# Mixer of a hybrid decoder step: state cleared in the projection phase, the norm's root one chunk earlier, and the scan's filling work in another order

## The reference

```python
zxbcdt = x @ w_in                                  # z, x/B/C, dt
xbc = silu(causal_conv(xbc, ...))                  # width 4, per channel
y, h_final = ssd_scan(xh, dt, a, bmat, cmat, h0)   # chunks of 128 tokens, state carried on
y = (y + d_skip * xh) * silu(z)
y = y * rsqrt(mean(y * y over the group) + eps) * norm_g
return y @ w_out
```

## Time and profile before

| what | us |
|---|---|
| median of 3 runs | 3813.22 (3812.39 to 3816.89) |
| the profiled execution | 3802.48 |
| its span, from the first to the last instruction | 3800.7 |
| PE busy | 3465.9 (91%) |
| DVE busy | 2221.5 (58%) |
| ACT busy | 973.7 (26%) |
| POOL busy | 997.9 (26%) |

### The profile page before, as it was taken

How to read it: one execution, slowest core, us unless ns; L and a number is a source line. 1 busy time by engine, 2 the same in 40 slices (tenths; PEclk the granted TensorE clock), 3 DMA queues, 4 the chain that set the end, 5 groups by cost and what they waited for, 6 DMA issues and landing times.

```text
span 3800.7 us, 55918 instructions
## 1 busy us (share of the span) xinstructions
PE 3465.9 (91%) x21178; PEld 3293.7 (87%) x21178; DVE 2221.5 (58%) x3463; ACT 973.7 (26%) x2300; POOL 997.9 (26%) x455
## 2 busy tenths in 40 slices
PE   7999999999996999999988888888886799999997
PEld 7888888888886999999987777777775699999997
DVE  7667767767767633333367666666666753333335
ACT  4333333433332211111113222322232211111112
POOL 3123222222211333433422111111110043333431
PEclk9999999999996999999988888888987799999997
DMA  3111111111110123211102220122110011111111
GB/s 113 36 40 59 48 40 59 42 40 59 42 42 27 45 89 134 89 51 45 45 34 75 62 61 33 44 66 61 61 50 28 12 51 45 45 50 45 45 50 51
DMA packets 85970, 200.85 MB, mean 53 GB/s; under 512 B 8920, under 2 KB 46808, under 8 KB 85248
## 3 DMA queue, kind: packets, MB, share of 16 engines
q1 hardware_dynamic: 35552, 139.54, 10.5%
q10 hardware_dynamic: 50224, 58.37, 4.9%
HBM read 166.93 MB, written 39.60 MB: 54 GB/s over the span
## 4 chain that ended last, share of the span: by engine, by line
issue 65%; PE 19%; POOLq 9%; POOL 5%; SPq 1%; DMA 0%; DVE 0%; ACT 0%; ACTq 0%; DVEq 0%
PE jb L342 19%; POOLq L317 8%; POOL wl L318 5%; SPq L297 1%; DMA wraw<-in_wstream 0%; PE aux L516 0%; ACT acc L937 0%; DVE acc L1346 0%; POOLq L325 0%; POOLq L314 0%; SPq L274 0%; SPq L280 0%; DVE lnq L1350 0%; ACT lnq L925 0%; PE aux L523 0%
## 5 line engine op out<-in xcount | busy, mean ns | idle before, releaser
L315 POOL TENSOR_TENSOR wh<-wraw,one 128x1024 fp32r<-128x1024 f32 x225 | 438.1, 1947 | 2705.7 <-PE jb L342 2253.2
L342 PE MATMUL jb<-xh,wh 128*128 128x344 f32 x2784 | 905.7, 325 | 25.0 <-issue 13.1
L342 PE MATMUL jb<-xl,wh 128*128 128x344 f32 x2784 | 892.4, 321 | 0.0
L342 PE MATMUL jb<-xh,wl 128*128 128x344 f32 x2784 | 892.1, 320 | 0.0
L1162 DVE TENSOR_TENSOR acc<-jb,acc 128x344 f32<-128x344 f32 x672 | 336.3, 515 | 473.2 <-PE jb L342 467.1
L318 POOL TENSOR_TENSOR wl<-wraw,wh 128x1024 fp32r<-128x1024 f32 x225 | 559.6, 2487 | 32.0
L342 PEld LDWEIGHTS jb<-xh,wh 128*128 128x128 f32 x2784 | 526.4, 189 | 33.3 <-issue 20.8
L342 PEld LDWEIGHTS jb<-xl,wh 128*128 128x128 f32 x2784 | 526.0, 189 | 1.7
L342 PEld LDWEIGHTS jb<-xh,wl 128*128 128x128 f32 x2784 | 526.0, 189 | 0.0
L342 PE MATMUL jb<-hh,wh 128*128 128x344 f32 x1536 | 492.2, 320 | 0.0
L342 PE MATMUL jb<-hl,wh 128*128 128x344 f32 x1536 | 490.9, 320 | 0.0
(11 more groups left out here) (251 smaller groups left out, 5658.4 us busy)
## 6 DMA issues: line engine op xcount, KB each, us to landing
wraw<-in_wstream SPq DMA_DIRECT2D x225, 512.0 KB, 3.2
pre<-in_state ACTq DMA_DIRECT2D x16, 512.0 KB, 4.2
out_ssm_s<-pre ACTq DMA_DIRECT2D x16, 512.0 KB, 3.2
kgat<-in_cache_k SPq DMA_DIRECT2D x16, 512.0 KB, 5.4
vgat<-in_cache_v SPq DMA_DIRECT2D x16, 512.0 KB, 6.4
past<-kgat ACTq DMA_DIRECT2D x8, 1024.0 KB, 5.7
past<-vgat ACTq DMA_DIRECT2D x8, 1024.0 KB, 5.9
acc<-in_xT SPq DMA_DIRECT2D x8, 516.0 KB, 7.2
```

The source lines that it names most:

```text
L315: nc.gpsimd.tensor_tensor(wh[slot][:].rearrange("p k m -> p (k m)"), wraw[:, slot].rearrange("p k m -> p (k m)"), one[:].to_broadcast([P, ...
L342: last = mm(jb[:, c, 0:CW], w[slot][:, j * kt + k], x[:, k, cols], start=(k == 0 and p == 0), stop=(k == kt - 1 and p == 2))
```

## The change

Three edits, all in the mixer.

1. Copying the group's decay factors and clearing the state `hst` (with the wait for the store of the state before) move from the head of DVE's `scan_group` to its `project_group`, behind the silu of chunk 3, at x == 4.
2. The root (ACT) and the reciprocal (DVE) of the norm move from x == 7 to x == 6. PE's part stays in its place.
3. In groups 1 to 7 the scan is filled with the six z chunks in steps 0 to 2, two each, and with the eight output blocks in steps 3 to 7 (two, one, two, two, one). Before, the output blocks stood in steps 0 to 2 (two, four, two) and the z chunks in steps 3 to 7. The stream is fetched in the new order. Group 0's filling stays.

```diff
-FILL = {0: (("o", 0), ("o", 1)), 1: (("o", 2), ("o", 3), ("o", 4), ("o", 5)), 2: (("o", 6), ("o", 7)),
-        3: (("z", 0, 0),), 4: (("z", 0, 1),), 5: (("z", 0, 2),), 6: (("z", 1, 0), ("z", 1, 1)), 7: (("z", 1, 2),)}
+FILL = {0: (("z", 0, 0), ("z", 0, 1)), 1: (("z", 0, 2), ("z", 1, 0)), 2: (("z", 1, 1), ("z", 1, 2)),
+        3: (("o", 0), ("o", 1)), 4: (("o", 2),), 5: (("o", 3), ("o", 4)), 6: (("o", 5), ("o", 6)), 7: (("o", 7),)}
...
-GROUP_ORDER = (0, 1, 2, 3, 4, 5, 6, 7)
+GROUP_ORDER = (0, 1, 2, 3, 6, 7, 4, 5)
...
-                        if x == 7 and fin:
+                        if x == 6 and fin:
                             norm_root(n - 1)
...
+            def begin_scan(n, fin):
+                nc.vector.tensor_copy(tg[:], tok[:, :, :, bass.ds(n * R, R)])
+                if fin:
+                    dve.wait_ge(s["h_out"], 16 * n)
+                nc.vector.memset(hst[:], 0.0)
+                drain().then_inc(s["h_zero"], 1)
...
                     if x:
                         silu(n, x - 1)
-                    if x == 7 and fin:
+                    if x == 4:
+                        begin_scan(n, fin)
+                    if x == 6 and fin:
                         invert(n - 1, "rms_sqrt", "rms_inv")
...
             def scan_group(at, n, out):
-                nc.vector.tensor_copy(tg[:], tok[:, :, :, bass.ds(n * R, R)])
-                if out:
-                    dve.wait_ge(s["h_out"], 16 * n)
-                nc.vector.memset(hst[:], 0.0)
-                drain().then_inc(s["h_zero"], 1)
```

## The result

The kernel before took 3815.05 us on the chip of the comparison (median of four runs, 3812.39 to 3821.64), the changed one 3854.44 us (median of four, 3843.27 to 3863.43). The ratio is 1.0117 with an interval of 1.0088 to 1.0145: the change costs 39.4 us, where the forecast had 20.9. The profiled executions took 3802.48 and 3843.27 us (spans 3800.7 and 3840.7), a difference of 40.8. One execution of the kernel before, on the chip where n1, a3, a4 and b1 ran, took 13767 us and is left out.

What follows compares the result with a forecast made beforehand. TensorE was taken to set the mixer's pace, its idle time a few recurring gaps per group. Added 77.7 less removed 56.8 gave +20.9 us, so 3823.4 profiled and 3834.1 predicted, range 3795 to 3856.

Steps and rivals of the forecast that it cites:

- L449 gone: Scan's first off-diagonal product no longer waits for the cleared state: 3.36 us per group, 23.5 us removed.
- L404 gone: The norm's spread no longer waits for the reciprocal, as the root moves earlier: 1.34 us per group, 9.4 removed.
- late bank gone: Projection: banks ScalarE frees late come in time without a z chunk in the last step; 5.9 us removed.
- wait at L432: Scan's first matmul waits for silu 9, delayed by GpSimd's split in the projection: 1.7 us (0 to 2).
- wait at L470: Scan's step 0: masked decay late after the split holds conv 11 and two silus; 2.0 us (0.5 to 3.5).
- gap ahead of o1 in step 3: VectorE's add frees the bank late, behind z gate, sample decay and GpSimd's split: 4.9 us, 5.3 at most.
- o pairs: Steps 5 and 6, two output blocks each: bank freed after it is wanted, 0.2 us each, 2.8 in all.
- loop's turn: TensorE's gap at the loop's turn, 1.25 us, was to stay as it is.
- clock at the removed wait: Slow clock (0.50) behind the wait for the cleared state goes with it: 2.1 us per group, 14.7 removed.
- covered entry: Rival: at the scan's entry conv 8 or conv 11 slips past the split, 25.9 us not added: 3808; chance 0.17.
- faster: Rival: the split's holds don't bite in step 3 either; 3772 with a covered entry; chance 0.18.
- the short gaps cost clock too: Rival: one of the new 1.7 and 2.0 us gaps leaves a slow clock, 15 us more: 3849; chance 0.13.

Runs made afterwards that it cites:

- n1: Changed kernel with the norm's root and reciprocal back at x == 7; 150.46 us per group against the changed kernel's 148.34.
- a3: Changed kernel with the split signal of the z unit in step 0 given in the middle of its second chunk; 146.63 us per group against 148.34.
- a4: Changed kernel with the split signal of the projection's last unit 2.4 us later; 150.06 us per group against 148.34.
- b1: Changed kernel with three late split signals, sample products a step earlier, second z gate, stores and output blocks moved; 3756.61 us against 3813.65 before, ratio 0.9844.
- a2: Changed kernel with the split signal of the o unit in step 3 given at its first block's third chunk; 145.93 us per group against 148.34.
- b3: The rebuilt kernel (b1) with all three split signals at their units' first matmul again; 139.46 us per group against 133.49.
- a1: Changed kernel with the sample states' stores behind ScalarE's last wait of the scan; 146.77 us per group against 148.34.
- p2: Kernel before with only the new filling and weight order; 150.41 us per group against 140.14 before.
- b5_split_later_x3: The rebuilt kernel (b1) with the last projection unit's split signal 1.0 us later; 133.30 us per group against 133.49.

## Why the prediction was right in its direction and wrong in its size

By its own steps, per group of the loop (us; a wait's price without the clock):

| step | forecast | measured |
|---|---|---|
| L449 gone | -3.36 | -3.36 |
| L404 gone | -1.34 | -1.34, by the filling, not by the root's move |
| late bank gone | -0.99 | -0.99 |
| wait at L432 | +1.7 | +1.82 |
| wait at L470 | +2.0 | +0.79 |
| gap ahead of o1 in step 3 | +4.9 | +4.75 |
| o pairs | +0.4 | +0.08 |
| loop's turn | 0 | +2.32 |
| clock at the removed wait | -2.1 | -2.28 |
| clock at the scan's entry | 0 | +2.36 |
| clock at step 3 | +2.1 | +2.19 |
| clock at the loop's turn | 0 | +1.88 |
| sum | +3.3 | +8.2 |

The clock's rows are TensorE's work at 0.50 in that part of the group (4.96 us before; 5.12, 4.76 and 4.09 after) times the 0.46 of the fit.

**Right.** The direction, and the three waits with what ends them. Step 3's gap was worked out instruction by instruction, and hit within 0.15 us. The entry's holds came as reckoned, 3.9 us on conv 8. The rivals "covered entry" and "faster" fell: the split got in between the two sample decays. This agrees with the exclusive lock of the Trainium skill (SBUF — State Buffer, Who interferes with whom), and a2, a3 and b3 show it by moving the split away.

**The step that failed first: the slow clock.** The prediction charged it behind one new wait only, 2.1 us for 2.1 removed. That charge was right (2.2 and 2.3), and so was the rival "the short gaps cost clock too", with its price: 7 x 2.36 = 16.5 us at the entry, where it had 15. The turn's 1.9 us stood nowhere. In all the work at 0.50 grew by 13.97 - 4.96 = 9.0 us, at 0.46 each 4.1 us per group, about 29 us over seven, where the prediction had nothing net.

The prediction leaned on group 0 for the short gaps, "a wait of 1.6 us left a stretch at 0.50". Its records say less. The clock was at 0.50 from 86.55 on, 0.9 us before that wait began (87.41 to 89.00):

```profile
86.55:87.40 0.85, 0.85 (x5) 0.46 (x3) 0.78 (x4) 0.00 (x0) 0.00 (x0) 0.50 0.00 0
```

What the length of a wait says can be counted over the fourteen traces, groups 1 to 6:

| wait of TensorE, us | waits | with a stretch at 0.50 that begins in it or up to 2.7 us behind it |
|---|---|---|
| 0.5 to 0.9 | 15 | 11, all at L470 of step 0 |
| 0.9 to 1.6 | 84 | 1 |
| 1.6 to 2.2 | 39 | 23 |
| 2.2 to 3.2 | 32 | 30 |
| over 3.2 | 96 | 96 |

So the length alone does not decide, and what must stand ahead of a short wait for the clock to fall behind it, these runs don't settle. The Trainium skill (TensorE: Matmul & The Clock Gate, Why this matters for your kernels) warns of long idle gaps between bursts; the last row agrees, and the row of 1.6 to 2.2 us goes against leaving out short ones.

**The term that was missed: the loop's turn.** The sentence "1.25 us at the loop's turn, which stays" was wrong by 2.32 us of idle time per group, and by the 1.9 us of clock that came with it, some 25 us over six turns. The change shortens step 7's fill, and so brings the stores ahead of the branch and takes the branch's cover; the prediction said of step 7 only that 18 matmuls cover the masked decay. Of the turn's growth a1 shows 1.22 as the stores; the other 1.10 I put down to the shorter fill, which agrees with b1 (fill of 36, turn 1.16) but was not tried alone.

**A size that was off the other way.** L470 was forecast at 2.0 and measured 0.79. The masked decay came 9.2 us into the fill (816.63 against 807.43), forecast 9.4 or a little more. But the fill itself ran 8.4 us instead of 7.8, since a part of it was at 0.50: the slow clock hid a wait. Where no stretch fell into step 0 (all of a4, four groups of n1, two of a2), the wait was 2.3 to 2.5 us. So this error and the first are one.

**A wrong reason for a right number.** L404's 1.34 us go without the root's move (p2, n1). I read it so that the last step no longer leaves VectorE behind, which agrees with the late bank that goes with it in p2; it was not tried by itself.

In sum, of the 4.9 us per group that were missing from the forecast, 4.1 are clock and 2.3 the turn, less 1.2 at L470 and 0.3 at the pairs. Six periods at 8.2 make 49.2 us; group 7's scan and the mixer's end add 4.0 and group 0 gives 0.9, in all the mixer's 52.3. The measured 39.4 is nearer to the forecast than these steps are, because the two profiled executions differ by 12.3 us the other way in stages that the change doesn't touch; that is luck.

## What to carry to other kernels

A wait on the pacing engine can be the cover of the next one: before removing it, lay out what starts earlier with it (here a split that holds VectorE), since the same edit cost 5.5 us per group alone and gained 4.6 once the splits' signals, the sample work and the stores had moved. On this TensorE, put the clock on top of each new wait of some 2 us or more (here 1.9 us at the turn, 2.2 at step 3, 2.4 at the entry); waits of 0.9 to 1.6 us went without (83 of 84), but at one place in the program, L470 of step 0, waits of 0.7 to 0.8 us did not (11 of 12). A slow stretch can also hide the next wait, which comes out when the first is removed (a4). When the last piece of a loop's body gets shorter, look at the branch: what covered it, and which transfers now start just ahead of it.

## What the runs showed of the hardware beyond that

- A loop's branch on TensorE took 3.3 to 3.7 us, with a packet of 16 KB of instructions that started 1.0 us after it began, and 4.7 to 4.9 us with two stores of 512 KB issued 0.4 us ahead of it and 0.1 us behind its start, the packet then starting after 2.4 us. Stores issued 2.8 and 2.4 us ahead left it at 3.7 to 3.8.
- Eleven of twelve waits of 0.7 to 0.8 us at one place (L470 of step 0) had a stretch of 3.41 us at 0.50 behind them, while 83 of 84 waits of 0.9 to 1.6 us had none; TensorE-busy time at 0.50 cost 0.46 us per us, over fourteen kernels.
- A VectorE instruction on 128x8 elements took 1.86 us instead of 0.22 when GpSimd's split had started 0.07 us ahead of it: its size does not shorten the hold.
- Moving a split by 1.0 us freed one VectorE instruction and held the next, 1.76 us lost for 1.70 (b5_split_later_x3).
